# x read channel-major and multiplied unnormalised, with a row of 1/rms applied by VectorE at eviction

## The reference

```
h = rms_norm(x, norm_mix_pre)          # x * rsqrt(mean(x*x, over channels) + eps) * g
z = h @ w_in                           # 1024 -> 5376 columns
qa, ka, va, qx, pin, gl = split(z)     # window attention, memory attention, pooling, gates
gates = sigmoid(gl)
...
mkv = rms_norm(mem, norm_mem) @ w_mem_kv
merged = gates[0]*ya + gates[1]*yx + gates[2]*yp     # three token mixers
x = x + rms_norm(merged @ w_out, norm_mix_post)
...                                                  # then a SwiGLU FFN, sandwich-normed
```

## Time and profile before

| what | value |
|---|---|
| median of 3 executions | 803.94 us (803.89 to 804.21) |
| the profiled execution's own time | 803.75 us |
| its span | 802.0 us |
| granted TensorE clock, mean | 0.999 |
| PE, DVE, ACT, POOL busy | 791.6, 455.7, 353.8, 46.9 us |

### The profile page before, as it was taken

How to read it: one execution, slowest core, us unless ns; L and a number is a source line. 1 busy time by engine, 2 the same in 40 slices (tenths; PEclk the granted TensorE clock), 3 DMA queues, 4 the chain that set the end, 5 groups by cost and what they waited for, 6 DMA issues and landing times.

```text
span 802.0 us, 11669 instructions
## 1 busy us (share of the span) xinstructions
PE 791.6 (99%) x4648; PEld 690.7 (86%) x4648; DVE 455.7 (57%) x550; ACT 353.8 (44%) x603; POOL 46.9 (6%) x99
## 2 busy tenths in 40 slices
PE   8999999999999999999999999999999999999997
PEld 8988778777777888888888999999999999888885
DVE  5743546566424523515655589888888887833222
ACT  5833545555446223324443455444444445632111
POOL 1100001144000000000001110000000000000000
PEclk9999999999999999999999999999999999999999
DMA  9831221312311333323471013333333344631011
GB/s 296 253 115 61 76 82 54 105 54 55 103 53 53 106 105 105 105 84 135 149 262 54 12 42 105 106 105 105 105 105 105 105 131 157 226 142 53 0 53 52
DMA packets 67925, 83.66 MB, mean 104 GB/s; under 512 B 3488, under 2 KB 61360, under 8 KB 67888
## 3 DMA queue, kind: packets, MB, share of 16 engines
q1 hardware_dynamic: 67712, 83.13, 31.8%
q10 hardware_dynamic: 176, 0.01, 0.0%
HBM read 81.02 MB, written 2.11 MB: 104 GB/s over the span
## 4 chain that ended last, share of the span: by engine, by line
PE 90%; DVE 4%; ACT 1%; DMA 1%; issue 1%; POOL 1%; SPq 0%; DVEq 0%; POOLq 0%; ACTq 0%
PE pair L1306 84%; PE pair L1423 1%; DMA raw<-in_w_mem_kv 1%; PE pair L1437 1%; PE pair L1404 1%; PE pair L1412 1%; PE pair L1442 1%; ACT probs L682 1%; POOL B_f L644 1%; DVE T_f L1193 1%; DVE op_lo L1173 1%; DVE T_lo L1200 0%; PE pair L1321 0%; PE pair L1338 0%; PE pair L1313 0%
## 5 line engine op out<-in xcount | busy, mean ns | idle before, releaser
L401 DVE TENSOR_TENSOR w_lo<-raw,w_hi 128x1024 fp32r<-128x1024 f32 x66 | 83.1, 1261 | 104.3 <-ACT w_hi L396 104.3
L1306 PE MATMUL pair<-hT_hi,w_hi 128*128 128x512 f32 x336 | 135.6, 403 | 0.0
L1306 PE MATMUL pair<-hT_hi,w_lo 128*128 128x512 f32 x336 | 131.2, 390 | 0.0
L1306 PE MATMUL pair<-hT_lo,w_hi 128*128 128x512 f32 x336 | 130.9, 390 | 0.0
L396 ACT ACTIVATE w_hi<-raw 128x1024 fp32r<-128x1024 f32 x66 | 69.6, 1056 | 97.6 <-PE pair L1306 81.0
L1306 PE MATMUL pair<-T_hi,op_hi 128*128 128x256 f32 x320 | 90.6, 283 | 0.5 <-DVE op_lo L1173 0.5
L1306 PE MATMUL pair<-T_lo,op_hi 128*128 128x256 f32 x320 | 90.6, 283 | 0.0
L1306 PE MATMUL pair<-T_hi,op_lo 128*128 128x256 f32 x320 | 90.6, 283 | 0.0
L1306 PEld LDWEIGHTS pair<-hT_hi,w_hi 128*128 128x128 f32 x336 | 63.1, 188 | 14.2 <-issue 1.0
L1306 PEld LDWEIGHTS pair<-hT_lo,w_hi 128*128 128x128 f32 x336 | 63.2, 188 | 13.4 <-issue 1.0
L1306 PEld LDWEIGHTS pair<-hT_hi,w_lo 128*128 128x128 f32 x336 | 63.1, 188 | 13.5
(11 more groups left out here) (191 smaller groups left out, 1553.2 us busy)
## 6 DMA issues: line engine op xcount, KB each, us to landing
raw<-in_w_in SPq DMA_DIRECT2D x42, 512.0 KB, 4.8
raw<-in_w_ffn_up SPq DMA_DIRECT2D x22, 512.0 KB, 4.8
raw<-in_w_ffn_gate SPq DMA_DIRECT2D x22, 512.0 KB, 4.2
raw<-in_w_ffn_down SPq DMA_DIRECT2D x22, 512.0 KB, 4.0
raw<-in_w_branch_a SPq DMA_DIRECT2D x8, 512.0 KB, 4.0
raw<-in_w_out SPq DMA_DIRECT2D x8, 512.0 KB, 3.7
raw<-in_w_mem_kv SPq DMA_DIRECT2D x6, 512.0 KB, 6.6
x_in<-in_x SPq DMA_DIRECT2D x4, 512.0 KB, 8.2
```

The source lines that it names most:

```text
L401: eng.tensor_tensor(lo, raw_view(s), hi.bitcast(F32), ALU.subtract).then_inc(weights_split, 1)
L1306: ins = pe.matmul(dst, a, b, start=first and n == 0, stop=last and n == 2, skip_group_check=onto)
```

## The change

x is given twice: as before (`x`), and channel-major (`x_t`, from the host's side, as mem already is). The channel-major form is loaded in the old places of the queue into `xT_in`, split with the gain into `hT_hi` and `hT_lo` from SBUF by ACT and DVE at s = 1 to 5 (`X_HI`, `X_LO`), and multiplied without 1/rms. No x is turned on PE.

The row form `x_in` is still needed for the squares. It lies on the same SBUF bytes as `xT_in` (both at 128 KB), so SP waits until all eight `_lo` tiles of x are made, then loads it, and only then goes on to chunk 5 (the weights of steps 10 and 11). ACT sums the four blocks' squares at s = 8, POOL makes 1/rms, DVE makes four diagonal matrices at s = 9, and PE multiplies them by ones at the end of step 9, which gives a [128, 512] tile in which every row is 1/rms. DVE copies it to SBUF (`x_rows`) at s = 10. Every tile that comes from x (k, v, 8 q, 4 qx, 4 pin, 24 gates) is now taken out of PSUM by DVE, multiplied by that row, where ACT copied it. After step 40 the row is moved to another place. `X_SCALE` of the old text, a constant of attention, is only renamed.

```diff
-X_SQUARES = {1: (0,), 3: (1,), 4: (2,), 5: (3,)}
-X_NORMS = {2: (0,), 4: (1,), 5: (2, 3)}
-X_TURNS = (6, 7)
+X_HI = {1: (0,), 3: (1,), 4: (2,), 5: (3,)}
+X_LO = {2: (0,), 4: (1,), 5: (2, 3)}
+X_SQUARES = 8
+X_SCALE = 9
...
+    xT_in = sb("xT_in", 128, [P, KT, SEQ])
     x_in = sb("x_in", 128, [P, TT, D])
...
-            def load_x(t):
-                sp.dma_start(x_in[:, t, :], x[P * t:P * t + P, :]).then_inc(x_loaded[t], 16)
+            def load_x(i):
+                sp.dma_start(xT_in[:, 2 * i:2 * i + 2, :], x_t[:, 2 * i:2 * i + 2, :]).then_inc(xT_loaded[i], 16)
...
-            for c in range(4, 6):
-                load_chunk(c)
+            load_chunk(4)
+            sp.wait_ge(turned_split, KT)
+            for t in range(TT):
+                sp.dma_start(x_in[:, t, :], x[P * t:P * t + P, :]).then_inc(x_loaded[t], 16)
+            load_chunk(5)
...
-            def turn_hi(e):
-                act.wait_ge(rows_turned, e + 1)
-                act.activation(turned_at(e, True), bk(4 + e % 4), ACT.Copy, scale=g_pre_c[:, e:e + 1]).then_inc(turned_hi, 1)
+            def x_hi(e):
+                act.activation(turned_at(e, True), xT_in[:, e, :], ACT.Copy, scale=g_pre_c[:, e:e + 1]).then_inc(turned_hi, 1)
...
-                for t in X_SQUARES.get(s, ()):
-                    act.wait_ge(x_loaded[t], 16)
-                    mean_square(x_in[:, t, :], NORM_X + t, square0[:, :])
...
+                for i in X_HI.get(s, ()):
...
+                    x_hi(2 * i)
+                    x_hi(2 * i + 1)
+                if s == X_SQUARES:
+                    for t in range(TT):
+                        act.wait_ge(x_loaded[t], 16)
+                        mean_square(x_in[:, t, :], NORM_X + t, square0[:, :])
...
+            def scaled_take(t):
...
+                src, row = bk(bank_of[n]), x_rows[tile_step[t] > ROW_MOVES]
+                dve.wait_ge(tile_full, n + 1)
+                if kind == "k":
...
+                    for g in range(GROUPS):
+                        for half in range(2):
+                            ins = dve.tensor_tensor(k_dup[64 * half:64 * half + 64, g, CHUNK:],
+                                                    src[64 * g:64 * g + 64, :], row[64 * g:64 * g + 64, :], ALU.mult)
...
+                elif kind == "pin":
+                    if i >= 2:
+                        dve.wait_ge(pool_diff_ready, i - 1)
...
+                dve.tensor_tensor(dst, src, row, ALU.mult).then_inc(tile_copied, 1)
...
-                for t in X_NORMS.get(s, ()):
-                    dve.wait_ge(rstd_ready, NORM_X + t + 1)
-                    dve.tensor_scalar(x_in[:, t, :], x_in[:, t, :], rstd[:, NORM_X + t:NORM_X + t + 1], None, ALU.mult)\
-                       .then_inc(rows_normed, 1)
+                for i in X_LO.get(s, ()):
...
+                    x_lo(2 * i)
+                    x_lo(2 * i + 1)
+                if s == X_SCALE:
+                    for t in range(TT):
+                        dve.wait_ge(rstd_ready, NORM_X + t + 1)
+                        dve.tensor_scalar(x_diag[:, t, :], ident[:, :], rstd[:, NORM_X + t:NORM_X + t + 1], None, ALU.mult)\
+                           .then_inc(x_diag_ready, 1)
+                if s == X_SCALE + 1:
+                    dve.wait_ge(x_scaled, 1)
+                    dve.tensor_copy(x_rows[0][:, :], bk(SCALE_BANK)).then_inc(x_row_ready, 1)
+                    dve.wait_ge(x_row_ready, 1)
...
+                if s == X_SCALE + 1:
+                    scaled_take(("k", 0))
                 if s >= 1:
                     for t in steps[s - 1]:
+                        if t in copied_no and t[0] not in ("mem", "k"):
+                            scaled_take(t)
...
-                if s in X_TURNS:
-                    b = X_TURNS.index(s)
-                    for e in range(4 * b, 4 * b + 4):
-                        turn_x(e)
+                if s == X_SCALE:
+                    for t in range(TT):
+                        pe.wait_ge(x_diag_ready, t + 1)
+                        ins = pe.matmul(bk(SCALE_BANK)[:, P * t:P * t + P], ones[:, :], x_diag[:, t, :], start=True, stop=True)
+                    ins.then_inc(x_scaled, 1)
```

More of the change, by code:

```diff
@@ L283, in encoder_block @@
         x_loaded = [sem(f"x_loaded{i}") for i in range(TT)]
+        xT_loaded = [sem(f"xT_loaded{i}") for i in range(4)]
+        x_diag_ready, x_scaled, x_row_ready = (sem(n) for n in ("x_diag_ready", "x_scaled", "x_row_ready"))
         x_again = [sem(f"x_again{i}") for i in range(TT)]
@@ L435, in as4 @@
             return v.rearrange("p (j q) -> p j q", j=4)
+        tile_step = {t: i for i, group in enumerate(steps) for t in group}
+        ROW_MOVES, SCALE_BANK = 40, 6
         E_X = KT
@@ L612, in _ @@
                 pool.tensor_tensor(rstd[:, c:c + 1], meansq[:, c:c + 1], minus_half[:, :], ALU.pow).then_inc(mem_rstd_ready, 1)
-            pool.wait_ge(rows_turned, E_V)
+            pool.wait_ge(rows_turned, E_V - KT)
             for i in range(4):
@@ L638, in _ @@
             pool.wait_ge(out_full, TT)
-            pool.wait_ge(rows_turned, E_V + 2 * TT)
+            pool.wait_ge(rows_turned, E_V - KT + 2 * TT)
             for t in (1, 2):
@@ L689, in exps @@
                         ins = act.activation(flat[:, i, :], scores[:, i // 2, at:at + N_MEM], ACT.Exp,
[L690 removed]
+                                             bias=neg_max[:, i:i + 1], scale=HD_SCALE, accum_out=row_sum[:, i:i + 1])
                     ins.then_inc(exps_done, 1)
@@ L705, in take @@
                     act.activation(dst, src[:, 0:N_MEM], ACT.Copy).then_inc(tile_copied, 1)
[L706 to L728, removed]
                 elif kind == "map":
@@ L1314, in turn_to @@
                 ins.then_inc(rows_turned, 1)
-            def turn_x(e):
-                pe.wait_ge(rows_normed, TT)
-                if e >= 4:
-                    pe.wait_ge(turned_split, e - 3)
-                for t in range(TT):
-                    ins = pe.transpose(bk(4 + e % 4)[:, P * t:P * t + P], x_in[:, t, P * e:P * e + P], ident[:, :])
-                ins.then_inc(rows_turned, 1)
             def tile(t, s, midway=None):
@@ L1615 @@
             a = a.reshape(GROUPS, 2, 2, 2).transpose(2, 0, 3, 1)
-        a = np.ascontiguousarray(a)
-        arrays[f"in_{name}"] = a
-        args.append(nc.dram_tensor(f"in_{name}", a.shape, mybir.dt.from_np(a.dtype), kind="ExternalInput").ap())
+        forms = {f"in_{name}": a}
+        if name == "x":
+            forms["in_x_t"] = a.T.reshape(KT, P, SEQ).transpose(1, 0, 2)
+        for key, a in forms.items():
+            arrays[key] = a = np.ascontiguousarray(a)
+            args.append(nc.dram_tensor(key, a.shape, mybir.dt.from_np(a.dtype), kind="ExternalInput").ap())
     result = nc.dram_tensor("result", (SEQ, D), F32, kind="ExternalOutput").ap()
```

70 lines of the change are left out of this document (42 added, 28 removed).

## The result

The changed kernel takes 809.83 us (808.15 to 810.01, 4 executions) against 804.08 of the kernel before (803.89 to 804.64, 4 executions): a ratio of 1.0066, interval 1.0053 to 1.0079. The prediction was 806.1, at most 809.0. The direction was right, the time was not. The profiled execution is the 808.15 one, the fastest of the four, with a span of 806.3 us, 4.3 more than before.

A forecast was written before the change was run, and what follows sets the result against it. The prediction took PE's list of matmuls as the bound. The profiled 803.75 us plus 2.2 for q0 starting later (a 4.8 us stall against a 2.6 gain) gave 805.95, 806.1 as median; range 804.8 to 809.0.

The forecast's parts named there:

- The wait for the diagonals: At the products ending step 9, ahead of q0: PE's longest wait, 3.5 to 4 us.
- the one at `mem_sum`: PE would wait about 1.3 us at `mem_sum` for DVE's sums, made behind lo(10).
- v's take: At step 10 on DVE: v copied at 54.9, wanted by PE at 55.3, a thin slack of 0.4 us.
- 3.3 us: Two blocks of x transposes leave PE's list, so step 8 starts 3.33 us earlier.
- 44.97: Start of q0 (step 10) without any wait, against 47.56 before: a gain of 2.6 us at most.
- A: Stall in front of q0, with the clock staying at its level: 806.1 us; chance 0.45.
- B: Same stall with the clock at its lower level behind it, 2.0 us more: 808.1 us; chance 0.27.
- chunk 5 has landed ... 40.5: x and chunk 5, 3.15 MB at 375 GB/s from 31.9, landed by 40.5, when hi(10) can start.
- the last receipt: 0.2 us added after chunk 5's transfer at 40.3, giving 40.5.
- cost at nothing: Takes moved from ACT to DVE, 28 us of work, were priced at zero because DVE's idle time holds them.
- 805.95: Whole-kernel sum before the median's offset: profiled execution 803.75 plus 2.2 us for the later q0.
- C: The chain to 1/rms is hidden and the 2.6 us gain is had: 801.3 us; chance 0.04.

The follow-up runs named there:

- e3: Changed kernel with x_in in memory of its own, and squares, sums, diagonals, row copy and k's and v's takes ahead of their step's splits: 800.63 us, ratio 0.9956.
- e0: The changed kernel run again with no edit: 810.23 us (809.08 to 811.34), ratio 1.0073 to the kernel before.
- e2: Changed kernel with only x_in in memory of its own, loaded ahead of chunk 5, order on ACT and DVE unchanged: 804.66 us, ratio 1.0004.
- e1: Changed kernel with unread warming transposes on PE ahead of mem_sum (22) and of the four products (30): 809.13 us, ratio 1.0063.
- e7: e3 with six unused 128x1024 products on DVE ahead of the diagonals, making an empty gap on PE: 807.82 us.
- e8: e7 with 48 warming transposes on PE in the gap as well: 806.36 us (805.31 to 807.05).
- e5: Changed kernel with one line of SP moved, so chunk 5 is issued ahead of x_in: 801.29 us, ratio 0.9966.
- e4: Kernel before, transposes kept, with only the takes of k, v, q, qx, pin and gate moved from ACT to DVE: 803.22 us, ratio 0.9990.
- e6: Changed kernel with only e3's order on ACT and DVE; x_in still shared and loaded ahead of chunk 5: 802.12 us, ratio 0.9980.

## Why the prediction was wrong

**The direction and the chain held.** The wait for the diagonals, the one at `mem_sum` in front of it and their order are as forecast, and v's take did not bind. The transposes gave about their 3.3 us: step 8 starts at 33.29 in the changed kernel and at 36.19 before, though the first matmul of `mem` stands 0.50 later (9.43 against 8.93). With nothing to wait for, e3 starts q0 at 45.56 where 44.97 was said.

**The step that failed first is the choice of A over B**: "the stall, the clock stays", 0.45 against 0.27. What I held against B, that `mem_sum` cuts the gap in pieces of about 1.3 and 4, was wrong twice: the first piece was 2.5 us (5.2 in e0), and e2 shows the lower level behind one wait of 2.4 us, straight after `mem_sum`, which is shorter than the 4 that I had forecast myself. The price in B, 2.0 us, was about right. (The 6.17 of the earlier trace rows still has the 0.24 of drain in it that I had taken off the 1.91 of the earlier trace rows, so the rows give 1.8.) Measured: 1.6 to 1.9 by e1's trace, 1.5 by e7 and e8, 1.3 by e2. The Trainium skill (TensorE: Matmul & The Clock Gate, "Why this matters for your kernels") warns that after an idle gap between bursts of matmuls the clock goes back to half, and the trace agrees: 1.00 to 0.50 in mid-kernel. That B's 808.1 is the time of the profiled execution (808.15) is luck: B lacks both terms that follow, and there they nearly cancel.

**The second is the term "chunk 5 has landed ... 40.5".** Its readings are 42.05, 44.95 and 44.42 in the three profiles of this chain, and its two halves fail in different ones. SP's loads began at 31.66, 32.17 and 32.98, and not at 30.07: 1.6, 2.1 and 2.9 late. In the first, the splits of x ended at 31.6 because lo(7) started at 27.75 and not at the 26.22 of before; 0.5 of that is there at ACT's first split of `mem` (6.38 against 5.88), and ACT then waited 0.71 and 0.48 us for `raw` and `xT_in`. From SP's first issue to hi(10) I had 10.4 us, and it was 10.4, 12.8 and 11.4. So the flow was priced right in the first profile, and cost up to 2.4 us more in the others. (The 0.2 us for the last receipt comes from no row.) My range gave 0.5 for the start and the receipt and 0.5 for the rate. That this term sets much of the spread is shown by e3 and e5, where the diagonals no longer hang on it so closely and the spreads are 0.35 and 1.35 us.

**The third is the takes on DVE, "cost at nothing".** They are worth 1.07 us (e4). I had looked only for what DVE would lose at its own idle places, and wrote that PE waits for neither engine. But PE waited 0.8 us for `probs` before. Set side by side, the two timelines of PE part at two places between the first and the eighth unit, both at the transposes of `probs`: by 0.85 at 145.03 and by 0.22 at 175.32 (times of before). For the first, the rows show what changed. Before, timelines of PE, DVE and POOL:

```profile
145.03 1.10 PE L1423 MATMUL pair<-ident,probs 128*128 128x128 f32 x8 [0.62 <-DVE probs L989]
...
138.68 1.19 DVE L971 TENSOR_TENSOR sink_gap<-sink,row_max 128x8 f32<-128x8 f32 x1
...
138.56 1.29 POOL L633 TENSOR_TENSOR pooled<-pooled,pooled 128x512 f32<-128x512 f32 x1
```

After, of PE and DVE:

```profile
149.68 1.04 PE L1444 MATMUL pair<-ident,probs 128*128 128x128 f32 x8
...
144.11 0.17 DVE L987 TENSOR_TENSOR sink_gap<-sink,row_max 128x8 f32<-128x8 f32 x1
```

The same small instruction on the softmax's way lasts 1.19 us in this unit before and 0.17 in its seven others and in all eight of after and of e4. Only there does an instruction of POOL, on the tile of pin 0, run beside it. With the take on DVE, POOL gets that tile later, past this place: its first instruction on it starts at 146.23 after and at 136.46 before, 9.77 apart, where PE is 5.43 later. ACT's eight exponentials take 3.1 us in both, so it is not that they run faster. That POOL's instruction is what held DVE's is argued from this one coincidence; no run moves POOL's work alone. The gain is luck in so far as nobody placed POOL's work with this in view. The 0.22 at the second place is not followed further.

**The sum closes for the profiled executions.** 805.95 + 1.5 (chunk 5) + 1.6 (clock) - 1.1 (takes) = 807.95 against 808.15 measured. For e0: 805.95 + 4.4 + 1.9 - 1.1 = 811.15 against 811.34. The median, 809.83, is 1.7 above the profiled execution; e0 shows that the start and the landing can move the time by more than this, but the three other executions have no trace. Of the miss in the median (3.7 us) the term of chunk 5 is then the larger part, an estimated 3.2.

**Of the other rivals:** C (the gain is had) needed the diagonals at 44.2, and I gave it 0.04 because 3.15 MB can't move in 3.2 us. That holds for this order of the transfers. With chunk 5 first (e5) they end at 45.6, where PE arrives at 44.9, and the gain is there.

**What stays open:** why the flow of x and chunk 5 is sometimes interrupted (164 GB/s in one stretch of e0), and why hi(10) starts 0.7 us (first profile) to 2.4 us (e0) after the stretches have moved 3.15 MB (summed over the stretches of 1 us from 33 on). Some of these bytes can be of the transfers behind chunk 5: SP had issued the pool weights and chunk 6 by 39.2 in the first profile and by 41.9 in e0. The Trainium skill (DMA: Bandwidth & Descriptors, "Why a DMA increments its semaphore by 16 and not by 1") says that the engines of one transfer finish independently and the semaphore counts all of them. No run here shows it by engine.

## What to carry to other kernels

When a computation is moved off the bound engine but its result is wanted at a fixed place, write down what each queue has ahead of it, the SyncE queue first: one line in SP's list was worth 8.5 us here, more than twice what the change was for. Price a stall on PE with the clock behind it: 1.3 to 1.9 us here, behind waits of 2.4 to 5.2 us. Give a term that rests on the landing of a large transfer a range from more than one execution: it moved by 2.9 us between two profiles of one program. And when a tile is handed over later, look also at what the engine that reads it will now run beside.

## What the runs showed of the hardware

- The granted clock fell to the 1.2 GHz level within one wait of 2.4 us that followed `mem_sum` (e2: 0.86 in the stretch 46 to 47, then 0.50), and within or just behind the first wait in the changed kernel (2.5 us: 0.52 in the stretch 47 to 48; 5.2 us in e0: 0.61 in that stretch). It stayed at the 2.4 GHz level behind waits of 1.2 us (e6) and 1.5 us (e1, with transposes on both sides). How long PE waits does not settle the moment: in e7's wait of 4.7 us, which began at 44.9 as e2's did, the stretches still show 1.00 until 49.
- The lower level cost 1.3 us (e2), 1.5 (e7 against e8) and 1.6 to 1.9 (changed kernel against e1) between the first product and the end of step 10. Transposes that nobody reads, put into the stall, kept the upper level.
- A result that hangs on the landing of a transfer inherits its spread: the changed kernel spreads over 2.3 us in e0, e8 over 1.7 with the clock at its upper level, e3 over 0.35.
- Moving the takes to DVE, whose busy time rose from 455.7 to 481.5 us, made the units 1.07 us shorter. A 128x8 instruction of DVE lasted 1.19 us beside a 128x512 instruction of POOL and 0.17 us elsewhere.
